# Keys and queries of a hybrid decoder step in seven half-size products a pair, work moved to GpSimd, and stage ends that no longer wait for their last stores

## The reference

```
xn = rmsnorm(x);  u = xn @ w_in            # w_in has the columns of all that follows
q, k, v, fl = fox columns (8 heads of 64); logf = log_sigmoid(fl + b_f)
o_a = softmax(q k^T / 8 + c_q - c_k) v     # c = cumsum(logf); samples also see 2048 cached rows
r, k, v, low-rank parts = rwkv columns, each mixed with the token before
S_t = S_{t-1} * d_t - (S_{t-1} kk_t) (kk_t a_t)^T + v_t k_t^T ;  o_t = S_t r_t    # 8 heads
o_b = (groupnorm(o) + bonus) * g
x = x + (sig(gA) * (o_a @ p_a) + sig(gB) * (o_b @ p_b)) @ w_o
x = x + mixture of experts (32 experts in 4 groups, 2 per token);  y = rmsnorm(x)
```

## Time and profile before

| | us |
|---|---|
| median of 3 runs | 1637.89 (1634.53 to 1644.49) |
| the profiled execution | 1645.24 |
| its span, first to last instruction | 1643.5 |
| PE busy | 1514.0 (92%) |
| PE weight loads | 869.6 (53%) |
| DVE busy | 680.5 (41%) |
| ACT busy | 362.0 (22%) |
| POOL busy | 497.4 (30%) |

### The profile page before, as it was taken

One profiled execution on the slowest core, in us unless ns is written; L12 is line 12 of the kernel. 1 busy time (PEld: TensorE's weight loads), 2 busy tenths in 40 slices (PEclk: granted clock), 3 DMA queues, 4 the chain that ended last, 5 costly groups with the idle time before them and its releaser, 6 DMA issues. The chain is left out here.

```text
span 1643.5 us, 29192 instructions
## 1 busy us (share of the span) xinstructions
PE 1514.0 (92%) x12025; PEld 869.6 (53%) x12025; DVE 680.5 (41%) x1295; ACT 362.0 (22%) x711; POOL 497.4 (30%) x506
## 2 busy tenths in 40 slices
PE   7999998989999999999999999899999599999992
PEld 4664455455777787755667775444444233323320
DVE  4203144433268887651554333235384222222225
ACT  3002144454123332011211111112012111111122
POOL 3001055654323345415334320000227312222224
PEclk9999999999999999989999999899999799999996
DMA  6603298999531112454231214654401779999997
GB/s 232 231 35 115 80 325 321 374 354 347 173 134 59 58 66 82 114 153 112 71 71 49 60 43 159 238 218 141 192 39 52 288 275 412 402 397 398 403 335 248
DMA packets 111478, 322.88 MB, mean 196 GB/s; under 512 B 31576, under 2 KB 41240, under 8 KB 100688
## 3 DMA queue, kind: packets, MB, share of 16 engines
q1 hardware_dynamic: 83200, 246.45, 40.7%
q0 software_dynamic: 26848, 70.25, 13.1%
q10 hardware_dynamic: 1296, 4.29, 0.7%
HBM read 270.78 MB, written 58.02 MB: 200 GB/s over the span
## 5 line engine op out<-in xcount | busy, mean ns | idle before, releaser
L1718 PE MATMUL gate_p<-rows,gate_w 128*128 128x352 f32 x576 | 182.5, 473 | 0.0
L1718 PEld LDWEIGHTS gate_p<-rows,gate_w 128*128 128x128 f32 x576 | 109.7, 194 | 63.9 <-ACT u_rw L1868 5.1
L2616 PE MATMUL x_p<-wgu,rows 128*32 128x512 f32 (+1 forms) x640 | 124.7, 616 | 2.8 <-DMA wgu<-in_we_gu 1.4
L2616 PE MATMUL x_p<-late,rows 128*32 128x512 f32 (+1 forms) x640 | 122.6, 599 | 0.0
L1683 POOL DMA_DIRECT2D t_ring<-t_blocks x128 | 69.3, 549 | 121.0 <-DVE tt L1937 117.7
L462 POOL DMA_INDIRECT rows<-in_cache_kT,page_index x41 | 42.0, 1025 | 190.6 <-PE fox_b L518 102.4
L2593 POOL DMA_INDIRECT y<-obT,moe_ent x24 | 25.0, 1040 | 219.7 <-DVE obT L2643 204.1
L1312 PE MATMUL rw_pp<-rows,rw_w 128*128 128x264 f32 x384 | 88.9, 387 | 1.8 <-DVE u_rw L1452 1.8
L2634 ACT ACTIVATE rows<-h_p,vec 128x128 f32<-128x128 f32 x96 | 27.5, 369 | 246.1 <-PE h_p L2611 246.1
L1312 PEld LDWEIGHTS rw_pp<-rows,rw_w 128*128 128x128 f32 x384 | 72.5, 190 | 15.7 <-issue 3.6
L2643 DVE SCALAR_TENSOR_TENSOR obT<-x_p,moe_scales,late 128x1024 f32<-128x1024 f32 x24 | 30.8, 1284 | 115.0 <-PE x_p L2628 115.0
(11 more groups left out here) (532 smaller groups left out, 2872.0 us busy)
## 6 DMA issues: line engine op xcount, KB each, us to landing
wgu<-in_we_gu SPq DMA_DIRECT2D x16, 2048.0 KB, 12.5
late<-in_we_gu SPq DMA_DIRECT2D x16, 2048.0 KB, 10.0
wd<-in_we_down SPq DMA_DIRECT2D x16, 1024.0 KB, 8.7
late<-in_we_down SPq DMA_DIRECT2D x16, 1024.0 KB, 12.6
rows<-in_cache_kT SPq DMA_DIRECT2D x41, 256.0 KB, 5.2
y<-const SPq DMA_DIRECT2D x9, 1024.0 KB, 5.1
rows<-in_cache_v SPq DMA_DIRECT2D x34, 256.0 KB, 7.4
gate_rows<-u_rw SPq DMA_DIRECT2D x48, 176.0 KB, 1.8
```

The lines of the kernel that those rows point to most:

```text
L1718: mm = pe.matmul(out[:, 0:GATE_N], gw[:, j % 2, k, :], e.xnT[:, k, at], start=(k == 0), stop=(k == KD - 1))
L2616: mm = pe.matmul(gu[d][at:at + n, :], hT[:, d, k, at:at + n], wgu[u][:, k, :], start=(k == 0), stop=(k == KD - 1))
```

## The change

1. Stage 1: q and k blocks j 2 to 7 are made as three pairs of seven half-size products, 4 blocks of features by 2 quarters of the tokens each, in the manner of stage 2. GpSimd sums weights and makes `t1x`; VectorE makes `t3x`, `t2x` and `t4x`, where `t4x` is written over `lf` in `probT_d` and so waits for `lf_stored`; it stands ahead of the first sum of a pair in VectorE's program. The `lf` store is issued right after the spill of `xnT`. The forget columns are made after the first half product. The loads of the weights 6 and 7 wait for the first pair.
2. The values of the last 32 tokens are made in four column groups side by side, then summed by one product with a selection matrix.
3. Stage 2: for p > 0 the small products come one time later, and the head sums all at 23 + 10 p. For p 0 to 2 the scaling of `beta` and `alpha` goes to GpSimd (`scale`), after the weight sums of pair 2, at the end of pair 3, and after the weight sums of pair 5; ScalarE waits for it (`scaled`) before it writes those buffers again. The last pair's gate stores are issued after the other waits of SP, and the last of them is waited for in stage 3 (`front_tail`).
4. Stage 3: gains start one chunk later, `oaT` is loaded after unit 15, and the last gate store and the state's store are waited for in stage 4 (`scan_tail`), ahead of the load of the gains.

The diff, cut to its core:

```
@@ units
-    if _c < FRONT_GATES + 6:
-        UNITS.append(("gain", 2 * (_c - FRONT_GATES)))
+    if 0 < _c - FRONT_GATES <= 6:
+        UNITS.append(("gain", 2 * (_c - FRONT_GATES - 1)))
     UNITS.append(("gate", 3 * _c))
...
+OA_AFTER = 15
@@ stage_fox, SP
             for j in range(4, 2 * HP):
-                sp.wait_ge(made, j - 3)
+                if j < 6:
+                    sp.wait_ge(made, j - 3)
+                else:
+                    if j == 6:
+                        sp.wait_ge(lf_scaled, 1)
+                        sp.dma_start(e.lf_d.rearrange("h (p t) -> p h t", t=PAGE), lf).then_inc(lf_stored, 16)
+                    sp.wait_ge(s_made, 4)
+                    sp.wait_ge(made, made_of(0, P4))
                 sp.dma_start(w[:, j % 4], a["w_in"][j]).then_inc(w_loaded[j % 4], 16)
                 if j == 5:
                     sp.wait_ge(xn_ready, KD)
                     sp.dma_start(wv, a["w_v"]).then_inc(wv_loaded, 16)
                     sp.dma_start(e.xn_d, e.xnT).then_inc(spilled, 16)
@@ stage_fox, GpSimd
+            for q in range(len(PAIRS)):
...
+                if q:
+                    pool.wait_ge(made, made_of(q - 1, P4))
+                else:
+                    pool.wait_ge(xn_ready, 6)
+                pool.tensor_tensor(s1, a21, a22, ALU.add).then_inc(s_made, 1)
+                pool.wait_ge(s_made, 4 * q + 1)
+                pool.tensor_tensor(s2, s1, a11, ALU.subtract).then_inc(s_made, 1)
+                pool.tensor_tensor(a21, a11, a21, ALU.subtract).then_inc(s_made, 1)
+                if q == 0:
+                    pool.wait_ge(xn_ready, KD)
+                    pool.tensor_tensor(t1x, x12, x11, ALU.subtract).then_inc(t1_made, 1)
+                pool.wait_ge(s_made, 4 * q + 3)
+                pool.tensor_tensor(s4, a12, s2, ALU.subtract).then_inc(s_made, 1)
...
@@ stage_fox, TensorE
-            for j in range(2, 2 * HP):
...
-                project(j, e.xnT, range(KD)).then_inc(made, 1)
+            def half_product(q, i, weights, tokens):
+                out = bank_of(q, i)
+                for k in range(4):
+                    for c in range(2):
+                        mm = pe.matmul(out[:, c], weights[:, k, :], tokens[:, k, c * QN:(c + 1) * QN], start=(k == 0), stop=(k == 3))
+                mm.then_inc(made, 1)
...
+                half_product(q, P1, a11, x11)
+                if q:
+                    pe.wait_ge(qk_dve, RAW + 4 * q)
+                else:
+                    forgets()
+                    pe.wait_ge(qk_act, 2)
+                half_product(q, P2, a12, x21)
+                pe.wait_ge(s_made, 4 * q + 2)
+                pe.wait_ge(t_made, 2)
...
+                half_product(q, P6, s2, t2x)
+                pe.wait_ge(s_made, 4 * q + 3)
+                pe.wait_ge(qk_dve, RAW + 4 * q + 1)
+                half_product(q, P7, a21, t3x)
...
+            def sampled_values():
+                pe.wait_ge(v_kept, TT - 1)
+                for k0 in (0, 4):
+                    for q in range(4):
+                        mm = pe.matmul(fa[32 * q:32 * q + 32, 3], e.xnT[:, k0 + q, SEQ:NT], wv[:, k0 + q, :],
+                                       start=(k0 == 0), stop=(k0 == 4))
+                mm.then_inc(parts_made, 1)
@@ stage_fox, VectorE
+            dve.wait_ge(xn_ready, KD)
+            dve.wait_ge(qk_dve, RAW)
+            dve.tensor_tensor(t3x, x22, x12, ALU.subtract).then_inc(t_made, 1)
+            dve.wait_ge(t_made, 1)
+            dve.tensor_tensor(t2x, t3x, x11, ALU.add).then_inc(t_made, 1)
+            dve.wait_ge(t_made, 2)
+            dve.wait_ge(lf_stored, 16)
+            dve.tensor_tensor(t4x, x21, t2x, ALU.subtract).then_inc(t_made, 1)
...
+            for q in range(len(PAIRS)):
+                u11, u12, u21 = result(q, 0, 0), result(q, 0, 1), result(q, 1, 0)
+                dve.wait_ge(qk_act, 4 * q + 1)
+                dve.wait_ge(made, made_of(q, P2))
+                dve.tensor_tensor(u11, bank_of(q, P2), u11, ALU.add).then_inc(qk_dve, 1)
...
@@ stage_rwkv_front
-    at_z, at_a, at_s, at_b = ({t + 10 * p: p for p in range(HP)} for t in (13, 14, 16, 22))
-    at_grams = {55: 0, 59: 1}
+    at_z, at_a, at_s = ({t + 10 * p + (p > 0): p for p in range(HP)} for t in (13, 14, 16))
+    at_b = {23 + 10 * p: p for p in range(HP)}
+    at_grams = {56: 0, 59: 1}
...
-            store_gates(len(PAIRS) - 1)
...
             sp.wait_ge(x_back, 16)
             sp.wait_ge(l_stored, 16 * 16)
+            store_gates(len(PAIRS) - 1)
+            sp.wait_ge(gate_stored[0], 16 * (FRONT_GATES // 2))
+            sp.wait_ge(gate_stored[1], 32 * (FRONT_GATES // 2) - 16)
...
+            def scale(p):
+                pool.wait_ge(exps, 2 * p + 1)
+                pool.wait_ge(cum_ready, p + 1)
+                pool.tensor_tensor(e.beta[:, p], e.beta[:, p], t2[:], ALU.mult).then_inc(scaled, 1)
+                pool.wait_ge(exps, 2 * p + 2)
+                pool.tensor_tensor(e.alpha[:, p], e.alpha[:, p], t1s[p % 2][:], ALU.mult).then_inc(scaled, 1)
...
                 weight_sums(q)
+                if q in (2, 5):
+                    scale((q - 2) // 3 * 2)
...
+                if q == 3:
+                    scale(1)
...
                     act.wait_ge(pair_done, p)
+                    act.wait_ge(scaled, 2 * p - 1)
                 act.wait_ge(shifted, 3 + 2 * p)
                 act.activation(t2[:], e.gamma[:, p], ACT.Square, scale=e.v("k_k")[:, p:p + 1]).then_inc(sq_done, 1)
@@ stage_rwkv_scan, SP
-            sp.dma_start(e.oaT, e.oa_d).then_inc(oa_back, 16)
...
+                if n == OA_AFTER:
+                    sp.dma_start(e.oaT, e.oa_d).then_inc(oa_back, 16)
...
-            sp.wait_ge(stored, 16)
             sp.wait_ge(oa_back, 16)
@@ stage_mix, SP
             load_a(3)
+            sp.wait_ge(e.scan_tail, 32)
             sp.dma_start(gain[:], e.gate_d[2 * KD:].rearrange("h p n -> p h n")).then_inc(gain_loaded, 16)
```

More of the change, by code:

```diff
@@ L555, in _, with forgets @@
-            mm.then_inc(f_made, 1)
+            def half_product(q, i, weights, tokens):
[4 more added lines that the diff above has]
+                mm.then_inc(made, 1)
+            def forgets():
+                pe.wait_ge(wf_loaded, 16)
+                pe.wait_ge(xn_ready, KD)
+                pe.wait_ge(qk_dve, RAW)
+                for k0 in (0, 4):
+                    for c in range(3):
+                        for q in range(4):
+                            mm = pe.matmul(fb[32 * q:32 * q + 32, c, 0:N3], wf[:, k0 + q, :],
+                                           e.xnT[:, k0 + q, c * N3:(c + 1) * N3], start=(k0 == 0), stop=(k0 == 4))
+                mm.then_inc(forgets_step, 1)
@@ L562, in values_of @@
                 n = size(t)
+                if t == TT:
+                    pe.wait_ge(v_kept, t)
+                    pe.wait_ge(select_set, 3)
+                    pe.wait_ge(parts_kept, 1)
+                    pe.matmul(fb[0:n, 3], select[:], v_parts, start=True, stop=True).then_inc(v_made, 1)
+                    return
                 for k in range(KD):
@@ new lines, in _, with sampled_queries @@
+            dve.wait_ge(qk_dve, RAW)
[5 more added lines that the diff above has]
+            dve.tensor_tensor(t4x, x21, t2x, ALU.subtract).then_inc(t_made, 1)
+            def sampled_queries():
+                dve.wait_ge(qs_zero, 1)
+                for s in range(2):
+                    for p in range(HP):
+                        col = (2 * p + s) * TS
+                        dve.tensor_copy(qs[half(s), :, p, col:col + TS],
+                                        qk[half(s), p, SEQ:NT].rearrange("p (b t) -> p b t", t=TS)).then_inc(qs_ready, 1)
@@ L1222, in _ @@
                     pool.wait_ge(pair_done, 3)
+                    pool.wait_ge(scaled, 2 * HP - 2)
                     pool.wait_ge(t_made, 4)
@@ L1248, in lower_grams @@
                 pe.wait_ge(pair_done, HP)
+                pe.wait_ge(scaled, 2 * HP - 2)
                 if g:
```

213 lines of the change are left out of this document (139 added, 74 removed).

## The result

The changed kernel takes 1649.64 us (median of 20 runs, 1644.74 to 1656.9) against 1642.88 us for the kernel before (20 runs beside them, 1634.51 to 1651.0): a ratio of 1.005, 95% interval 1.0034 to 1.0065. The forecast, 1627.3 against 1637.89, was a ratio of 0.9935. So by the ratio the change costs some 8 us (0.5% of 1643) where I had it gain 10.6.

What follows compares the result with a forecast made beforehand. TensorE, busy 92% of the span, bounds the kernel. 4.5 - 4.0 - 10.0 - 1.1 = -10.6 us took the profiled 1645.24 to 1634.6, or 1627.3 against the runs' median; own range 1618 to 1635, with most of rivals 1 and 2 1612 to 1638.

Steps and rivals of the forecast that it cites:

- Stage 1, +4.5: Stage 1: products and sampled values save time, but waits ahead of P7 cost more; +4.5 us (+1 to +11).
- The argument from one queue in order: Stage 1: the lf store, behind w_v and the spill in SP's queue, lands 1.4 us behind the spill, at 73.8.
- Stage 2, -4.0: Stage 2: later small products shorten head-sum waits, and scaling moved to GpSimd costs nothing; -4.0 us (0 to -9).
- gains of 2.0 for p = 1 and 0.4 for p = 3: Stage 2 head sums: VectorE's last five steps meet GpSimd's weight sums less for p = 1, as much for p = 3.
- The six multiplications moved to GpSimd: Stage 2 scaling: takes VectorE's time off stretches where it waits anyway; priced at nothing, 3.6 us each without cover.
- Stage 3's start, -10.0: End of stage 2 and start of stage 3: earlier fills and ring, no lower clock behind; -10.0 us (-6 to -13).
- the 7.5 us at `across(0)`: Start of stage 3: ring ready ahead of TensorE, which is through at 755.9 instead of 763.36; 7.5 us gained.
- End of stage 3, -1.1: End of stage 3: without the last store's wait, VectorE's last sums set the end; -1.1 us (0 to -2).
- The 0.7 us for the end of stage 2: End of stage 2: the last store is no longer waited for; 0.7 us gained (0 to 1.9).
- 1 and 2: Rivals: 1, lf store does not hold TensorE, total -23.7, chance 0.12; 2, ring not earlier, total -1.3, chance 0.13.
- Rival 3: Stage 2: GpSimd becomes the bound, ScalarE stops copying products and TensorE stops; +8.4 us, 1646.3, chance 0.09.
- The 7.3 us: Base: the median of the runs lies 7.3 us below the profiled execution, turning 1634.6 into 1627.3.

Runs made afterwards that it cites:

- stage 1 alone: Kernel before with the changed kernel's stage 1 and nothing else: 1647.61 us, ratio 1.0023 to the kernel before.
- the tails alone: Kernel before with only the waits for the last stores of stages 2 and 3 moved to the stage behind: 1642.15 us, ratio 0.9989.
- the scan alone: Kernel before with stage 3's changes only (gains a chunk later, oaT after unit 15), stage ends as before: 1643.01 us, ratio 0.9986.
- `oaT` first: Changed kernel with oaT loaded at the start of stage 3 as before, new unit order kept: 1659.53 us, ratio 1.0092 to the kernel before.
- that order alone: Changed kernel with t4x made behind VectorE's sum with P2 of the first pair: 1640.24 us, ratio 0.9983 to the kernel before.
- the early store and the stage 2 of before: Changed kernel with lf stored ahead of the spill, stage 2's times and scaling as before; with t4x later too: 1627.01 us, 0.9897 of before.

## Why the prediction was wrong

**Stage 1, +4.5: right.** The scores came 4.9 us later in the profile of after, 3.8 us were measured with stage 1 alone. P7 was forecast at 77.0 and started at 77.06 (TensorE's idle time ahead of it was 14.7 us and not 17.0: the forget columns took 5.45 us and not 3.7, but VectorE set P7's start), the first values at 142.7 and 142.96; the last tile of values to the scores took 4.6 us, from 204.17, where it had been 8.0: 3.4 saved, 3.6 forecast. The argument from one queue in order (weights 1.2 us behind the spill) carried it.

**Stage 2, -4.0: the step that failed.** It measured +7.4 (the two intervals leave some 4 us either way). Two sentences of it are at fault.
- "One product later is worth 3.56 us, but only for p = 0 is the rest of the chain unmoved: 1.6 us gained." The head sum's wait did go. I had looked at what it waits for, not at what the product moved ahead of it waits for: the bank that a `combine` frees, behind the same chain. Before, that wait was hidden under the head sum's own 1.9 us and nothing in the list of waits showed it. For p > 0 I had gains of 2.0 for p = 1 and 0.4 for p = 3. The wait of p = 1 (2.93) went altogether and that of p = 3 fell from 3.06 to 2.63, but the head sum of p = 2, which had waited for nothing, now waited 1.64, and new waits on `combine` and ScalarE's copies (0.5 to 1.6 each) took the place. The times also lengthen the stage's end: 4.0 to 4.4 us of wait in all kernels with the new times, 2.3 to 2.5 in those with the old times and the rest of after. It was 3.6 in the kernel before and with the tails alone, 3.8 and 4.0 with stage 1 and the scan alone. So some 1.8 us of the 7.4 lie at the stage's end; which engine ends last there, and what besides the tails brings 2.3, I have not settled.
- "The six multiplications moved to GpSimd take VectorE's time off stretches where it waits anyway ... priced at nothing." VectorE did not wait there: in the kernel before it made the four multiplications of p = 0 from 512.7 to 518.1 in the middle of a stretch, 485.7 to 521.8, in which its only gap is 0.19 us; those of p = 1 and 2 lie in stretches without one (535.0 to 566.1, 600.9 to 613.0). What was moved came back as blocked time behind GpSimd's slower multiplication. By the medians it cost 1.3 us alone, and 3.1 with the new times (1.005 against 1.0031), neither beyond its interval; that VectorE's stretch is longer for it, 7.4 us against 5.3, the rows show.

**Stage 3's start, -10.0: mis-sized.** The mechanism is shown by the run with `oaT` first. In the profiled pair stage 3 took 311.2 us before and 302.6 after, 8.6 less, close to the 10.4 of my terms for stage 3 (the stage end's 0.7 left out, the 1.1 at its end in). But the same code as before took 305.9 in the kernel with stage 1 alone, where the ring wait was 0.96 us and not 3.55 and no clock was lost behind it, and the runs give 2.3 us for the scan. With the tails alone stage 3 took 303.4, against 299.9 to 303.1 in the nine kernels with the tails, the new order and `oaT` behind unit 15. I had sized the gain on a wait seen once. Of the 7.5 us at `across(0)` 6.2 came (58.2 against 64.5), and behind it the waits in the second and third chunk gave some back (0.9 each in after).

**End of stage 3, -1.1: right.** The wait ahead of the mix went from 2.50 to 1.26 us, and is the same in every kernel with the tails. The 0.7 us for the end of stage 2, in the same edit, did not come: 3.59 before, 3.62 with the tails alone, 4.11 in after.

**The rivals.** 1 and 2 did not come: `lf` held, and the ring was early. Rival 3 had the sign, and its +8.4 us is near the +8.2 measured, but by luck and not by its mechanism: no product of after waited over 0.8 us for ScalarE's copies; GpSimd did not become the bound but slowed the engine that was. So the cause of stage 2's loss stands in none of my cases. By the sum of the measured parts, +3.8 for stage 1, +7.4 for stage 2, -2.3 for the scan and -1.8 for the tails make +7.1, against +8.2 measured; each part is uncertain by some 3 to 4 us.

**The base.** The 7.3 us between the profiled execution and the median of three runs was 2.4 against twenty; as a ratio this cancels.

## What to carry to other kernels

When a step is moved behind another, ask what the other waits for and whether it is released by the same chain; a wait that is hidden under the moved step stands in no list. Look at the engine that both wait for: if it runs without a gap, moving one wait only moves it to the next product, unless TensorE gets other work to do meanwhile. Work given to GpSimd can come back as VectorE's time at the shared port. And place an instruction that waits for a DMA behind all that does not need it: here that order alone was worth 11 us by the medians (8.8 at the scores), and with the early store and the stage 2 of before it made the change worth 1.0%.

## What the runs showed of the hardware that was not expected

- A copy of 16 columns on VectorE took 2.39 us beside a multiplication of 1056 columns on GpSimd, and 0.16 without it; `t4x` (2112 columns) took 6.71, 3.40 and 2.36 us by what GpSimd did beside it.
- "issue" in a row of TensorE has two faces. Ahead of the forget columns it was 3.58 us and ended 0.1 us behind VectorE's last piece of `xnT` (47.28 + 5.82 = 53.10, start 53.20): a semaphore's wait without its name. In the scan it stood in the middle of groups of like matmuls, up to 3.7 us, most often 24 to 27 and 85 to 93 us behind `across(0)`, and each time TensorE went on 1.25 to 1.57 us behind the end of a 16 KB load of instructions. Waits of the second kind make one profile a poor witness for differences of 2 to 3 us.
- A transfer of 2112 KB held small transfers of other queues: the first four 128 KB pieces of the lower blocks took 13.3 us beside it and 6.1 in after, where it came later, and a chunk's ring load was late enough for a wait of 5.94 us.
